# Three output tiles behind three norms, multiplied feature tile by feature tile, and splits kept up to them

## What is computed

```python
def swiglu(u, w_in, w_out):
    a, b = jnp.split(u @ w_in, 2, axis=-1)
    return (jax.nn.silu(a) * b) @ w_out

def first_block(...):
    ...
    u = modulate(rmsnorm(h, g_norm_mix[l]), sh2, sc2)
    h = h + gt2 * token_mixing(u, ...)
    u = modulate(rmsnorm(h, g_norm_ffn2[l]), sh3, sc3)          # n2, then w2
    h = h + 0.5 * gt3 * swiglu(u, w_ffn2_in[l], w_ffn2_out[l])
    return rmsnorm(h, g_final)                                   # nf

def ffn_sublayer(x, shift, scale, gate, w_in, w_out, ln_g, ln_b):
    y = swiglu_2(modulate_2(x, shift, scale), w_in, w_out)       # f0 behind nf, f3 behind l11
    return layer_norm(ALPHA * x + 0.5 * gate * y, ln_g, ln_b)
```

## Time and profile before

| | us |
|---|---|
| median of 3 runs | 2620.17 |
| lowest, highest | 2618.76, 2622.85 |
| the profiled execution: its time | 2622.8 |
| its span, first to last instruction | 2621.0 |
| PE busy | 2491.6 |
| DVE busy | 1863.1 |
| ACT busy | 1104.2 |
| mean granted clock of PE, as a share of 2.4 GHz | 0.973 |

### The profile page before, as it was taken

The page is one execution under the profiler, slowest core; times in us unless marked ns, Lnnn a source line. Parts: engine busy times, 40 slices in busy tenths (PEclk is TensorE's granted clock), DMA queues, the critical chain, the costliest instruction groups (busy, mean ns, idle before and its releaser), DMA issues.

```text
span 2621.0 us, 39392 instructions
## 1 busy us (share of the span) xinstructions
PE 2491.6 (95%) x15574; PEld 2253.0 (86%) x15574; DVE 1863.1 (71%) x3600; ACT 1104.2 (42%) x1650; POOL 0.2 (0%) x4
## 2 busy tenths in 40 slices
PE   4998999989999999999999999999999999998998
PEld 3998989889989888787888898888998888877998
DVE  6987977778879545677887569897785444576656
ACT  3444565444453323734223572222552222645443
POOL 0000000000000000000000000000000000000000
PEclk8998999989989999999999999999999999898999
DMA  8986756758858432454443166676374332222663
GB/s 305 310 265 196 257 193 200 253 179 262 294 182 260 138 97 65 157 181 133 145 147 124 63 188 206 193 233 193 97 269 133 113 105 94 72 66 76 189 187 104
DMA packets 161383, 453.68 MB, mean 173 GB/s; under 512 B 17712, under 2 KB 21296, under 8 KB 161200
## 3 DMA queue, kind: packets, MB, share of 16 engines
q1 hardware_dynamic: 161200, 451.16, 53.4%
HBM read 450.04 MB, written 1.05 MB: 172 GB/s over the span
## 4 chain that ended last, share of the span: by engine, by line
PE 61%; DVE 4%; ACT 3%; issue 1%; DMA 0%; ACTq 0%; SPq 0%; DVEq 0%
PE PS L1116 19%; PE PS L1117 19%; PE PS L1118 19%; PE PS L1258 1%; ACT own L1323 1%; DVE own L1586 1%; PE PS L1141 1%; PE PS L1143 1%; PE PS L1304 0%; DVE X L1682 0%; DVE X L1568 0%; PE PS L1287 0%; ACT NT L1382 0%; DVE Ul L1686 0%; ACT Uh L1378 0%
## 5 line engine op out<-in xcount | busy, mean ns | idle before, releaser
L1586 DVE TENSOR_TENSOR own<-raw,own 128x1024 fp32r<-128x1024 f32 x425 | 518.3, 1221 | 315.2 <-ACT own L1323 312.9
L1116 PE MATMUL PS<-Uh,own 128*128 128x256 f32 (+1 forms) x2064 | 658.1, 319 | 44.4 <-DVE Ul L1671 22.5
L1117 PE MATMUL PS<-Ul,own 128*128 128x256 f32 (+1 forms) x2064 | 645.2, 313 | 0.0
L1118 PE MATMUL PS<-Uh,own 128*128 128x256 f32 (+1 forms) x2064 | 644.9, 312 | 0.0
L1323 ACT ACTIVATE own<-raw 128x1024 fp32r<-128x1024 f32 x425 | 443.1, 1053 | 343.4 <-PE PS L1118 311.0
L1116 PEld LDWEIGHTS PS<-Uh,own 128*128 128x128 f32 x2064 | 399.3, 193 | 77.5 <-issue 37.2
L1117 PEld LDWEIGHTS PS<-Ul,own 128*128 128x128 f32 x2064 | 400.9, 194 | 20.0 <-issue 0.2
L1118 PEld LDWEIGHTS PS<-Uh,own 128*128 128x128 f32 x2064 | 400.6, 194 | 20.2
L1116 PE MATMUL PS<-Hh,own 128*128 128x256 f32 (+1 forms) x1096 | 351.1, 320 | 5.0 <-DVE Hl L1818 3.6
L1117 PE MATMUL PS<-Hl,own 128*128 128x256 f32 (+1 forms) x1096 | 345.9, 316 | 0.0
L1118 PE MATMUL PS<-Hh,own 128*128 128x256 f32 (+1 forms) x1096 | 345.8, 316 | 0.0
(11 more groups left out here) (221 smaller groups left out, 3887.0 us busy)
## 6 DMA issues: line engine op xcount, KB each, us to landing
MODS<-in_mm SPq DMA_DIRECT2D x168, 256.0 KB, 3.6
SCR<-in_mm SPq DMA_DIRECT2D x136, 256.0 KB, 3.6
raw<-in_f0i SPq DMA_DIRECT2D x64, 512.0 KB, 3.7
raw<-in_f1i SPq DMA_DIRECT2D x56, 512.0 KB, 3.6
raw<-in_f2i SPq DMA_DIRECT2D x56, 512.0 KB, 3.5
SCR<-in_ma SPq DMA_DIRECT2D x88, 256.0 KB, 5.4
raw<-in_w1i SPq DMA_DIRECT2D x44, 512.0 KB, 4.6
raw<-in_w2i SPq DMA_DIRECT2D x44, 512.0 KB, 4.3
```

The costliest lines, as they stand in the source:

```text
L1116: e.matmul(o, ll, rh, start=start, stop=False)
L1117: e.matmul(o, lh, rl, start=False, stop=False)
L1118: return e.matmul(o, lh, rh, start=False, stop=stop)
L1586: e.tensor_tensor(low, raw[:, w.n % RING, :], high.bitcast(F32), ALU.subtract).then_inc(s["wlo"].tell(w.n), 1)
```

## The change

At n2, nf and l11, the first gate tile, the first up tile and the second gate tile of the following layer get their three banks together, and their products are put as eight steps `products`, one for each feature tile, each with that feature tile's nine matmuls (three weight tiles, three matmuls each). At nf and l11 they are put into the norm's loop, at n2, where the list of fillers isn't empty, behind it. The chunks are taken ahead of the norm's loop (behind it at n2), with the splits that belong to them. The evictions of the three tiles (`gate`, `up`, `gate`) follow all eight steps; their splits to `Hh` and `Hl` and the next `chunk` come behind. Beside that, `deep` stays set through the outputs of the last slab of a layer on the latents alone, so that splits go on there; the rate behind nf is 0.5 instead of 1.6, up to the point where it becomes 2.4; and the `flush` ahead of f0 is gone.

```diff
+    def feature_tiles(self, st, names):
+        first = len(self.stream)
+        for i, (name, j) in enumerate(names):
+            self.chunk(name, j, LEAD - i)
+        for i in range(len(names)):
+            self.used[first + i] = ("feature", first + i)
+        return dict(st=st, r=LAT, n=first, banks=tuple(self.bank(True) for _ in names))
...
-    def norm_tiles(self, what, site, t, r, fills, after, **fields):
+    def norm_tiles(self, what, site, t, r, fills, after, tiles=None, **fields):
+        first = self.feature_tiles(*tiles) if tiles and not self.filler else None
         for k in range(KT + 1):
             self.put(what, st=site, k=k, n=t["n"], r=r, after=after, **fields)
             if t["centred"] and k in (0, 2, 4):
                 self.centre(t, k + 2)
+            if first and k:
+                self.products(first, k - 1)
             if k < KT:
                 self.fill(fills[1])
         self.norming = False
+        if tiles and not first:
+            first = self.feature_tiles(*tiles)
+            for k in range(KT):
+                self.products(first, k)
+        return first
...
+    def ffn_tiles(self, st):
+        return (st, [(st + "i", 0), (st + "i", FT), (st + "i", 1)])
+
+    def begin_ffn(self, st, t):
+        j = self.pairs
+        self.pairs += 2
+        self.of_feature("gate", t, 0, st + "i", f=0, j=j)
+        self.of_feature("up", t, 1, st + "i", f=0, j=j)
+        self.hidden(st, 0, slots_of(SLABS)[0], j, t["r"])
+        self.of_feature("gate", t, 2, st + "i", f=1, j=j + 1)
+        self.gated[st, 1, t["r"]] = j + 1
...
         n = len(slabs) - 1
-        self.deep = False
         if r is BOTH:
+            self.deep = False
             self.outer_halves(st, w_out, firsts[n], slabs[n], n + at, [slots[f] for f in slabs[n]], norm)
         else:
             yield from out(n, norm)
+            self.deep = False
...
-    p.rms("n2", 0, 6, "g2", (3, 1), nm_last)
+    p.begin_ffn("w2", p.rms("n2", 0, 6, "g2", (3, 1), nm_last, 0, p.ffn_tiles("w2")))
     p.rate = 0.85
-    p.drain(p.ffn("w2", "w2o", LAT, [(("w2", 0), "half", 0, 8)], False))
+    p.drain(p.ffn("w2", "w2o", LAT, [(("w2", 0), "half", 0, 8)], False, early=1))
...
-    p.norm_tiles("fin", "nf", t, LAT, (2, 1), w2_last)
+    p.begin_ffn("f0", p.norm_tiles("fin", "nf", t, LAT, (2, 1), w2_last, p.ffn_tiles("f0")))
     for k in range(KT):
         p.put("finscale", k=k)
-    p.rate = 1.6
+    p.rate = 0.5
     p.fill(1000)
-    p.flush()
...
+                elif w.what == "products":
+                    for i, b in enumerate(w.banks):
+                        on.wait_ge(s["wlo"], w.n + i)
+                        if w.k == 0:
+                            claim(b)
+                        u_ready(w.st, w.k, w.r)
+                        m = three(PS[:, b[0], lo:hi], *weights(w.n + i, w.k), Uh[:, w.k, lo:hi], Ul[:, w.k, lo:hi],
+                                  w.k == 0, w.k == KT - 1)
+                        if w.k == KT - 1:
+                            m.then_inc(s["matmul"].tell(("feature", w.n + i)), 1)
```

More of the change, by code:

```diff
@@ L159, in __init__ @@
         self.squares = 0
+        self.gated = {}
         self.freed = {}
@@ L375, in norm_tiles, with rms @@
         self.norming = False
-    def rms(self, site, which, sec, gain, fills, after, ahead=0):
+        if tiles and not first:
[3 more added lines that the diff above has]
+        return first
+    def rms(self, site, which, sec, gain, fills, after, ahead=0, tiles=None):
         if not ahead:
@@ L385, in rms, with layer_norm @@
         self.mod_until(which, sec)
-        self.norm_tiles("rms", site, t, LAT, fills, after, q=which, f=sec)
-    def layer_norm(self, site, l, i, ll, sec, r, keep, fills, after):
+        return self.norm_tiles("rms", site, t, LAT, fills, after, tiles, q=which, f=sec)
+    def layer_norm(self, site, l, i, ll, sec, r, keep, fills, after, tiles=None):
         t = self.tallied(r, 1e-5, fills)
@@ L396, in layer_norm @@
         self.column((site, "s"), "shift", w, sec)
-        self.norm_tiles("ln", site, t, r, fills, after, q=w, f=sec, slab=li)
+        first = self.norm_tiles("ln", site, t, r, fills, after, tiles, q=w, f=sec, slab=li)
         if not keep:
-            return
+            return first
         if li not in self.scaled:
@@ L405, in layer_norm, with products, of_feature @@
             self.later(1 + k // 3, lambda k=k: self.put("rescale", st=site, k=k, r=r, slab=li))
+        return first
+    def feature_tiles(self, st, names):
[5 more added lines that the diff above has]
+        return dict(st=st, r=LAT, n=first, banks=tuple(self.bank(True) for _ in names))
+    def products(self, t, k):
+        self.put("products", k=k, **t)
+    def of_feature(self, what, t, i, st, **fields):
+        self.put(what, st=st, n=t["n"] + i, r=t["r"], bank=t["banks"][i], after=("feature", t["n"] + i), **fields)
+        self.held.discard(t["banks"][i][0])
+    def ffn_tiles(self, st):
[8 more added lines that the diff above has]
+        self.gated[st, 1, t["r"]] = j + 1
     def project(self, name, i, st, what, r, **fields):
@@ L415, in ffn_in @@
     def ffn_in(self, st, f, q, r):
-        j = self.pairs
-        self.pairs += 1
-        self.project(st + "i", f, st, "gate", r, f=f, j=j)
-        yield
+        if (st, f, r) in self.gated:
+            j = self.gated[st, f, r]
+        else:
+            j = self.pairs
+            self.pairs += 1
+            self.project(st + "i", f, st, "gate", r, f=f, j=j)
+            yield
         self.project(st + "i", FT + f, st, "up", r, f=f, j=j)
@@ L543, in through, with product_key @@
         return w
+def product_key(w):
+    return w.after or (w.id, 0)
 def schedule(total):
@@ L662, in schedule @@
     p.column("ca_gf", "scaled", "gf")
-    p.norm_tiles("fin", "nf", t, LAT, (2, 1), w2_last)
+    p.begin_ffn("f0", p.norm_tiles("fin", "nf", t, LAT, (2, 1), w2_last, p.ffn_tiles("f0")))
     for k in range(KT):
         p.put("finscale", k=k)
-    p.rate = 1.6
+    p.rate = 0.5
     p.fill(1000)
-    p.flush()
-    p.drain(p.ffn("f0", "f0o", BOTH, [(("f0", 0), "half", 1, 2)], True, alone=ALONE, at=2, then={4: lambda: p.close(3)}))
+    p.drain(p.ffn("f0", "f0o", BOTH, [(("f0", 0), "half", 1, 2)], True, early=1, alone=ALONE, at=2, then={4: lambda: p.close(3)}))
     p.flush()
@@ L851, in schedule @@
     qk_last = max(w.id for w in p.order if w.what == "qk2"), 0
-    p.layer_norm("l11", 1, 1, 1, 6, LAT, True, (0, 0), qk_last)
-    p.drain(p.ffn("f3", "f3o", LAT, [(("f3", 0), "half", 3, 8)], True))
+    p.begin_ffn("f3", p.layer_norm("l11", 1, 1, 1, 6, LAT, True, (0, 0), qk_last, p.ffn_tiles("f3")))
+    p.drain(p.ffn("f3", "f3o", LAT, [(("f3", 0), "half", 3, 8)], True, early=1))
     p.flush()
@@ L1144, in tensor @@
                              stop=w.final, skip_group_check=True).then_inc(s["matmul"].tell(("sums", w.n, w.k)), 1)
+                elif w.what == "products":
[8 more added lines that the diff above has]
+                            m.then_inc(s["matmul"].tell(("feature", w.n + i)), 1)
+                elif w.what in ("gate", "up", "pool_in", "qk1") and w.after:
+                    pass
                 elif w.what in ("gate", "up", "pool_in", "qk1", "sigmoid", "gu", "qk2"):
@@ L1400, in scalar @@
                 elif w.what == "gate":
-                    on.wait_ge(s["matmul"], (w.id, 0))
+                    on.wait_ge(s["matmul"], product_key(w))
                     if w.j >= 2:
```

## The result

The changed kernel takes 2614.9 us (median of 12 runs, 2613.7 to 2616.0), the kernel before on the same chip 2622.3 us (12 runs, 2618.8 to 2624.2). The ratio is 0.9974, with a 95% interval of 0.9965 to 0.9983: 7.4 us less, where 8.4 us less was forecast. The forecast time, 2611.8 us, is 3.1 us too low: 2.1 us because the median of the kernel before is 2622.3 us over twelve runs and not the 2620.17 us of the first three, 1.0 us because the change brought less. A second comparison on another chip gave 2613.2 against 2619.8 us, ratio 0.9974 again. The profiled execution took 2614.83 us, with a span of 2612.8.

What follows compares the result with a forecast made beforehand. PE bounds the kernel, busy 95% of the span and waiting at norms. Gains of 3.0 (n2), 3.9 (l11), 0.2 (nf) and 1.3 us (modulation) sum to 8.4, taking the 2620.17 us median to 2611.8; range 2604.5 to 2620.

Steps and rivals of the forecast that it cites:

- Clock after a gapless start: At n2, nf and l11: PE runs gapless, full clock 4.3 us after the first product, 72nd product after 10.4 us.
- Low part ahead of l11: Before l11's first multiply on DVE: one more weight tile's low part delays the first product by 1.15 us.
- Next weights in time: Behind the third tile at n2 and l11: queued splits take 2.9 us, PE needs them after 3.0 us; cost nothing.
- The ring in w2's closing outputs: Before nf: added splits stretch accumulate, square, high part, low part turns to 4.50, 3.80, 4.50 us; last accumulate 4.7 us later.
- nf as a whole: At nf: delay from w2's late outputs against the faster 72 products, net gain 0.2 us (ends 0.2 and 4.9).
- Rate: Behind nf: moving eighteen double modulation steps to later f0 removes PE's accumulate wait near 801.81, gain 1.3 us.
- Rival D: Between 880 and 892: moved modulation steps make PE wait, 5.5 us lost, 2617.3 us; chance 0.14 including similar losses.
- Three steps of four gone: Behind nf: three of four modulation steps leave, so PE's 1.25 us accumulate wait at 801.81 goes.
- B: Rival at w2's closing outputs: they aren't late, total gain 13.1 us, 2607.1 us; chance 0.16.
- C: Rival at the three norms: clock rises no sooner than before, change worth 0.5 us, 2619.7 us; chance 0.15.
- E: Rival at the three sites: three banks in turn keep PE at 1.2 GHz, 5.7 us slower, 2625.9 us; chance 0.06.
- the idle ahead of the norm's first tile: Before n2, nf and l11: PE idles 6.05, 5.29 and 6.15 us, which no reordering of products can touch.

Runs made afterwards that it cites:

- the edit alone: Kernel before with only the extra splits in w2's closing outputs (spare places kept full): 2626.5 us, +5.7 us against the kernel before.
- the edit undone: Changed kernel with the extra splits in w2's closing outputs taken out, spare places as before: 2611.9 us, -8.9 us against the kernel before.
- two tiles: Changed kernel with two tiles run feature by feature and the third tile behind them, at each site: 2613.0 us, -6.8 us against the kernel before.
- full spare places: Kernel before with two splits more at each of w2's closing output chunks, order and rates as before: 2626.5 us, +5.7 us.
- second group: Four kernels run on one chip with the kernel before (2619.8 us); the unaltered changed kernel took 2613.2 us there.
- the splits placed late: Changed kernel without the splits in w2's closing outputs, weight splits around nf and l11 reordered on ACT and DVE: 2608.4 us, -11.4 us against the kernel before.

## Why the prediction was right, point by point

The prediction was right in its time, in its mechanism and in most terms, and one term was mis-sized. That the total came within 1.0 us is in part chance: the terms missed by 1.9 us together, and 0.9 us came back (the sum, below).

- **Clock after a gapless start.** Forecast 4.3 us (2.6 to 5.2) from first product to rise, and 10.4 us to the 72nd. Measured over six profiled executions with the feature order and an idle stretch ahead of it (the changed kernel twice and four variants), eighteen sites: 2.9 to 6.1 us and 9.9 to 11.3 us to the 72nd. The mean, 4.25 us, is the forecast; the spread is wider than the three rows behind it showed, and n2 in the changed kernel, at 11.1 us, lies outside the 9.7 to 10.8 that was given. At n2 the gain was 2.3 us (forecast 3.0), at l11 5.2 less the delay (below) 4.0 (forecast 3.9).
- **Low part ahead of l11.** Forecast 1.15 us. DVE makes the low part and then the norm's first multiply, as in the rows below. PE's idle there is 7.29 against 6.15 us, 1.14 more, and with the low part behind the norm it is back at 6.15.

```profile
2402.59 1.22 DVE L1649 TENSOR_TENSOR own<-raw,own 128x1024 fp32r<-128x1024 f32 x1
2403.72 0.68 DVE L1745 TENSOR_TENSOR X<-X,RS 128x512 f32<-128x512 f32 x1
```

- **Next weights in time.** Forecast 0. In the 200 products behind each third tile of the changed kernel no two starts lie more than 0.19 us apart. At nf the cover was the early splits: without them, with the order alone, PE waits 3.00 us there.
- **The ring in w2's closing outputs.** Forecast turns of 4.50, 3.80, 4.50, measured 4.45, 3.78, 4.45. The mechanism is shown by the edit alone and by the edit undone. The last accumulate came 4.6 us later relative to n2's 72nd product (186.34 against 181.76), where 4.7 was forecast. The total was too small, though: nf's first product came 6.0 us later, not 4.7. This is the mis-sized term. I had let sums, root and norm follow the last accumulate unchanged. They don't. From last accumulate to the statistics it was 1.73 us (747.03 to 748.76) and is now 3.11 (748.25 to 751.36), 1.4 us more. In the kernel before, PE had outputs to multiply until 746.8 and stood at the higher clock. Now it has waited 4.71 us, its clock is at 0.50 from 747.7, and the second pair of sums starts 1.02 us behind the first (748.39, 749.41), where it was 0.43. The kernel with the splits undone has full clock there and 1.73 us again. Rows: the sums before, and the stretch of the sums now.

```profile
746.83 0.60 PE L1143 MATMUL PS<-NT,ones 128*128 128x256 f32 x2
747.26 0.59 PE L1143 MATMUL PS<-SQ,ones 128*128 128x256 f32 x2
...
747.70:751.40 3.70, 2.93 (x6) 1.85 (x6) 1.07 (x4) 0.83 (x2) 0.00 (x0) 0.50 0.81 257
```

- **nf as a whole.** Forecast a gain of 0.2, measured a loss of 1.3 us (10.66 against 15.31, less 6.0).
- **Rate.** Forecast 1.3 us, measured 1.5. Rival D, the moved steps coming out on PE, fell: DVE was full between 880 and 892 as worked out, and PE didn't wait. "Three steps of four gone" was too much: by the rates, 0.5 for 1.6, it is two of three, and the wait went all the same.
- **Rivals.** B fell (the ring was late), C fell (counted from the first product, the clock rose 3.1 us sooner than before at n2, 6.8 at nf and 8.0 at l11), E fell: with three banks in turn PE went to full clock at each site, and the rule of the Trainium skill that it rests on (TensorE: Matmul & The Clock Gate, A second HAM failure mode: psum-queue depth-cycling) is not seen here, with PE busy 4.90 of 4.90 us at 1.00 (557 to 561.9).
- **What it left out.** I wrote that the idle ahead of the norm's first tile can't be touched by reordering the products. That is so, but at n2 most of it was DVE's queue, and 8.1 us by the medians lay there, more than the whole change brought.
- **The sum.** Forecast -8.4 us, measured -7.4. The errors: -0.7 at n2, -1.5 at nf, +0.1 at l11, +0.2 behind nf, 1.9 us in all, and about 0.9 the other way that the medians have and the terms don't: chance, as far as is known.

## What to carry to other kernels

Where PE comes from an idle stretch into work that another engine hands over piece by piece, give each piece more products than PE does in its time at the lower clock: here that took 12 us off three sites. With two tiles the clock rose as soon as with three, and the medians lie 0.2 us apart. What is then made early to feed it must not go into a queue that sets the end ahead of it: the same splits cost 6 us between accumulate and square, and no wait of PE behind the norm's last row. Here an idle stretch of PE of 4.71 us also made the small work behind it slower, by 1.4 us, so a delay ahead of a serial chain can cost more than itself. And before the work behind an idle stretch is reordered, read what stands in the queue of the engine that ends the idle.

## What the runs showed of the hardware that was not expected

- The clock does not follow from the program alone. The changed kernel, run on two chips, had 0.50 from 1205.0 to 1208.5 us in one profiled execution (first row) and not in the other (second row):

```profile
1205.10:1208.40 3.30, 3.30 (x9) 2.53 (x9) 0.87 (x1) 3.29 (x5) 0.00 (x0) 0.50 0.02 5
```

```profile
1205.10:1208.40 3.30, 3.30 (x16) 2.70 (x15) 2.37 (x4) 2.33 (x3) 0.00 (x0) 1.00 0.03 5
```

  Of the twelve profiled executions, seven show a fall between 1194 and 1213 us and five don't; the kernel before and the changed kernel's first execution do, the kernel before with full spare places and the changed kernel's second don't.
- From the same idle and the same gapless run of products, the clock rose 2.9 us after the first product in one execution and 6.1 in another (n2 in the changed kernel of the second group and with the splits placed late). That is 1.4 us of the time at one site, and more than two tiles and three differ at any. The Trainium skill (TensorE: Matmul & The Clock Gate, Part 1: The HAM clock gate) gives this point a spread of half a microsecond either way from run to run; the eighteen sites here spread over 3.2 us, and for this kernel the measured spread decides.
- The place of n2's last product ahead of the idle, reached by one and the same program, lies between 542.5 and 548.8 us over eleven executions. So stages were compared by intervals between products and not by their times.
